# The forget gates' running sums as rows that are split once, and convolution blocks that start two accumulation banks later

## What is computed

```python
qkv = jax.nn.silu(causal_dwconv(jnp.concatenate([gq, gk, gv], axis=-1), gdn_conv[l]))
logf = jax.nn.log_sigmoid((ff + fox_fbias[l]).astype(f32))      # 256 tokens x 4 heads

def fox_attention(q, k, v, logf):
    c = jnp.cumsum(logf, axis=1).transpose(0, 2, 1)
    for i in range(S // Q_BLOCK):                               # two blocks of 128 queries
        s = einsum(q_block, k[:hi]) * scale + (c[:, :, lo:hi, None] - c[:, :, None, :hi])
        p = jax.nn.softmax(jnp.where(mask, s, -jnp.inf), axis=-1)
```

## Time and profile before

| | us |
|---|---|
| executions shown, lowest and highest undisturbed | 1149.84, 1151.31 |
| median shown | 1151.31 |
| the profiled execution, its own time | 1150.2 |
| its span, first to last instruction | 1148.5 |

### The profile page before, as it was taken

One profiled execution on the slowest core, in us unless ns is written; L12 is line 12 of the kernel. 1 busy time (PEld: TensorE's weight loads), 2 busy tenths in 40 slices (PEclk: granted clock), 3 DMA queues, 4 the chain that ended last, 5 costly groups with the idle time before them and its releaser, 6 DMA issues.

```text
span 1148.5 us, 16462 instructions
## 1 busy us (share of the span) xinstructions
PE 1137.1 (99%) x6408; PEld 993.3 (86%) x6408; DVE 741.6 (65%) x931; ACT 589.4 (51%) x788; POOL 105.7 (9%) x162
## 2 busy tenths in 40 slices
PE   9999999999999999999999999999999999999997
PEld 8998888888889999988888898899888888889885
DVE  6866686657777888754664554665866566545465
ACT  5674654446565766543554443564554364444353
POOL 6410211000011000000000000200500010000020
PEclk9999999999999999999999999999999999999999
DMA  9643753455634765564665656465457467555641
GB/s 252 206 156 97 223 185 110 164 201 184 217 132 138 251 207 176 187 215 147 209 214 182 186 174 209 154 213 181 145 187 239 146 229 234 192 168 175 213 137 72
DMA packets 122894, 209.81 MB, mean 183 GB/s; under 512 B 10965, under 2 KB 58186, under 8 KB 122827
## 3 DMA queue, kind: packets, MB, share of 16 engines
q1 hardware_dynamic: 119225, 198.64, 54.2%
q10 hardware_dynamic: 3506, 10.23, 2.4%
q0 software_dynamic: 96, 0.01, 0.1%
HBM read 207.67 MB, written 1.18 MB: 182 GB/s over the span
## 4 chain that ended last, share of the span: by engine, by line
PE 94%; DVE 3%; DMA 1%; ACT 1%; issue 0%; POOL 0%; POOLq 0%; DVEq 0%; SPq 0%; ACTq 0%
PE ACCP L867 28%; PE ACCP L869 28%; PE ACCP L868 28%; PE SMP L1068 3%; DVE CONVF L2301 1%; PE SMP L1061 1%; DVE LO L2176 1%; DMA RAW<-in_w_in_dram 1%; DMA X<-in_x_dram 0%; PE SMP L1221 0%; PE SMP L1237 0%; PE SMP L1021 0%; PE SMP L1016 0%; PE SMP L1015 0%; PE SMP L1406 0%
## 5 line engine op out<-in xcount | busy, mean ns | idle before, releaser
L2176 DVE TENSOR_TENSOR LO<-RAW,HI 128x1024 fp32r<-128x1024 f32 x365 | 438.1, 1237 | 231.3 <-ACT HI L1607 225.0
L1607 ACT ACTIVATE HI<-RAW 128x1024 fp32r<-128x1024 f32 x366 | 370.1, 1054 | 269.6 <-PE ACCP L869 222.6
L867 PE MATMUL ACCP<-HI,XH 128*128 128x512 f32 x704 | 277.4, 394 | 0.0
L869 PE MATMUL ACCP<-HI,XL 128*128 128x512 f32 x704 | 274.4, 390 | 0.0
L868 PE MATMUL ACCP<-LO,XH 128*128 128x512 f32 x704 | 274.0, 389 | 0.0
L867 PE MATMUL ACCP<-XH,HI 128*128 128x256 f32 x640 | 182.0, 284 | 0.7 <-DVE CONVF L2301 0.7
L869 PE MATMUL ACCP<-XH,LO 128*128 128x256 f32 x640 | 181.1, 283 | 0.0
L868 PE MATMUL ACCP<-XL,HI 128*128 128x256 f32 x640 | 181.1, 283 | 0.0
L869 PEld LDWEIGHTS ACCP<-HI,XL 128*128 128x128 f32 x704 | 132.1, 188 | 27.8
L868 PEld LDWEIGHTS ACCP<-LO,XH 128*128 128x128 f32 x704 | 132.3, 188 | 26.2
L867 PEld LDWEIGHTS ACCP<-HI,XH 128*128 128x128 f32 x704 | 132.3, 188 | 26.2
(11 more groups left out here) (416 smaller groups left out, 1144.5 us busy)
## 6 DMA issues: line engine op xcount, KB each, us to landing
RAW<-in_w_in_dram SPq DMA_DIRECT2D x104, 512.0 KB, 4.5
RAW<-in_w_up_dram SPq DMA_DIRECT2D x44, 512.0 KB, 4.4
RAW<-in_ffn_w_gate_dram SPq DMA_DIRECT2D x44, 512.0 KB, 4.6
RAW<-in_ffn_w_up_dram SPq DMA_DIRECT2D x44, 512.0 KB, 4.5
RAW<-in_ffn_w_down_dram SPq DMA_DIRECT2D x44, 512.0 KB, 4.4
RAW<-in_w_down_dram SPq DMA_DIRECT2D x22, 512.0 KB, 4.2
RAW<-in_w_out_dram SPq DMA_DIRECT2D x8, 512.0 KB, 4.4
RAW<-in_w_mkv_dram SPq DMA_DIRECT2D x8, 512.0 KB, 4.3
```

The source lines that it names most:

```text
L867: pe.matmul(dst, lhs[0], rhs[0], start=start, stop=False)
L869: return pe.matmul(dst, lhs[1], rhs[0], start=False, stop=stop)
L1607: act.activation(HI[:, n % RING, half_of(half)], RAW[:, n % RAWS, half, :], ACT.Copy).then_inc(hi_ready, 1)
L2176: dve.tensor_tensor(LO[:, s, c], RAW[:, n % RAWS, half, :], HI[:, s, c].bitcast(f32), ALU.subtract).then_inc(lo_ready[s], 1)
```

## The change

Three things, which don't depend on each other.

**Banks.** gdn block j now uses ACCP bank (j + 2) % 4, so that sbqk blocks 0 to 3 follow gdn blocks 2 to 5. The two products that spread the gain of the first norm go to banks 0 and 1 instead of 2 and 3, the idle spins to bank 2.

**Order on ACT and DVE.** ACT copies block j ahead of the silu of block j-1. DVE adds the taps of block 5 ahead of the LO of block 8; the LO of blocks 8 and 9 follow it.

**Running sums.** DVE builds, early, two small tiles: CUM_IN, log f twice (columns 0 to 3 and 32 to 35), and CUM_SEL, which for each head h has ones in rows h and 32+h. PE forms all running sums once, `fcum`, with two fp32 products behind the join that reads `Z16`. ACT rounds the 36 rows to f32r (CUM), and DVE overwrites rows 32 to 35 with the remainder. In the score stage each head's running sum is then one single-pass product of CUM_SEL (36 rows) with CUM. PE does all single-pass products of the three banks first, then the eight fp32 products of queries and keys. `fcum` is a new name in SMALL, so each name behind it moves one bank on; fS0, fS1a and fS1b now wait for Z16_1, fcum and Tt32_0 instead of Z16_0, Z16_1 and Tt32_0.

```diff
@@ _accumulations @@
-                acc(phase, j, j, (j + (phase == "up") * 2) % 4)
+                acc(phase, j, j, (j + (phase in ("gdn", "up")) * 2) % 4)
@@ SMALL @@
-SMALL += ["Z16_0", "Z16_1", "Tt32_0", "Tt32_1", "fS0", ...
+SMALL += ["Z16_0", "Z16_1", "fcum", "Tt32_0", "Tt32_1", "fS0", ...
@@ tiles @@
+        CUM, CUM_IN = at("CUM", 58, [P, SEQ], f32r), at("CUM_IN", 59, [P, NT, 36])
+        CUM_SEL = at("CUM_SEL", 80, [P, HEADS, P], f32r)
@@ PE @@
             t_half("gate_c", 2, XH, XL)
             join(16, 0)
+            pe.wait_ge(cum_in, 1)
+            small_bank_free(pe, "fcum")
+            pe.matmul(small("fcum")[0:36, 0:SEQ], CUM_IN[:, 0, :], flat(UPTO[:, :, :]), start=True, stop=False)
+            finish(pe.matmul(small("fcum")[0:36, P:SEQ], CUM_IN[:, 1, :], TRI, start=False, stop=True))
             t_half("gate_c", 3, XH, XL)
...
-            def fox_scores(name, t, heads):
+            def fox_bias(name, t, heads):
                 small_bank_free(pe, name)
                 n = (t + 1) * P
                 pe.matmul(by_head(small(name), n), IDENT_R[:, :], every(NEG_AFTER_R[:, SEQ - n:SEQ], len(heads)), start=True, stop=False)
                 for i, h in enumerate(heads):
-                    dst = small(name)[:, i * n:(i + 1) * n]
-                    pe.matmul(dst, FQK[:, h, tok(t)], FQK[:, 4 + h, 0:n], start=False, stop=False)
-                    last = pe.matmul(dst, TS[:, 0, h:h + 1].broadcast_to([P, P]), flat(UPTO[:, 0:t + 1, :]), start=False,
-                                     stop=t == 0 and h == heads[-1])
-                    if t == 1:
-                        last = pe.matmul(dst[:, P:SEQ], TS[:, 1, h:h + 1].broadcast_to([P, P]), TRI, start=False, stop=h == heads[-1])
+                    pe.matmul(small(name)[:, i * n:(i + 1) * n], CUM_SEL[0:36, h, :], CUM[0:36, 0:n], start=False, stop=False)
+
+            def fox_products(name, t, heads):
+                n = (t + 1) * P
+                for i, h in enumerate(heads):
+                    last = pe.matmul(small(name)[:, i * n:(i + 1) * n], FQK[:, h, tok(t)], FQK[:, 4 + h, 0:n], start=False,
+                                     stop=h == heads[-1])
                 finish(last)
+            small_is_taken(pe, "fcum")
+            for scores in SCORES:
+                fox_bias(*scores)
+            for scores in SCORES:
+                fox_products(*scores)
@@ ACT, gdn blocks @@
-                if j:
-                    conv_silu(j - 1)
                 acc_is_done(act, "gdn", Turn(j))
                 (two copies of block j)
+                if j:
+                    conv_silu(j - 1)
                 split_ahead("gdn", Turn(j))
@@ ACT, gate_c @@
             take_small("Z16_0", MB[0:112, 0, :, 0:64], by_head(small("Z16_0")[0:112, 0:256], 64))
+            small_is_done(act, "fcum")
+            copy(CUM[0:36, :], small("fcum")[0:36, 0:SEQ], cum_hi)
@@ DVE, gdn blocks @@
-                split_ahead("gdn", Turn(j))
+                if j < 4:
+                    split_ahead("gdn", Turn(j))
+            split_ahead("gdn", Turn(4))
+            split_ahead("gdn", Turn(5))
@@ DVE, behind the LO of block 19 @@
             split_ahead("foxqk", Turn(3))
+            link(dve.memset(CUM_IN[:, :, :], 0.0))
+            dve.tensor_copy(CUM_IN[:, :, 0:4], TS[:, :, 0:4])
+            dve.tensor_copy(CUM_IN[:, :, 32:36], TS[:, :, 0:4])
+            dve.tensor_tensor(CUM_SEL[0:36, :, :], IDENT[0:36, 0:4]..., IDENT[0:36, 32:36]..., ALU.add).then_inc(cum_in, 1)
             heads_norm(1, XS, 2 * HW)
@@ DVE, gate_c @@
             take_small("Z16_1", MB[0:112, 1, :, 0:64], by_head(small("Z16_1")[0:112, 0:256], 64))
+            dve.wait_ge(cum_hi, 1)
+            dve.tensor_tensor(CUM[32:36, :], small("fcum")[32:36, 0:SEQ], CUM[32:36, :].bitcast(f32), ALU.subtract).then_inc(bank_of("fcum"), 1)
             bias("c", 1)
```

More of the change, by code:

```diff
@@ L148 @@
 SMALL += ["kk0", "kk1", "kq0", "kq1", "z0", "z1", "z2", "z3", "rc0", "rc1", "rc2", "rc3", "so0", "so1", "T16_0", "T16_1", "fTq0", "fTq1", "fTk0", "fTk1"]
-SMALL += ["Z16_0", "Z16_1", "Tt32_0", "Tt32_1", "fS0", "fS1a", "fS1b", "Z32_0", "Z32_1", "T32_0", "T32_1"]
+SMALL += ["Z16_0", "Z16_1", "fcum", "Tt32_0", "Tt32_1", "fS0", "fS1a", "fS1b", "Z32_0", "Z32_1", "T32_0", "T32_1"]
 SMALL += ["Tt64_0", "Tt64_1", "fP0", "fP1a", "fP1b", "fo0", "fo1", "Z64_0", "Z64_1", "T64_0", "T64_1"]
@@ L398, in build @@
         row_max, probs_ready = sems("row_max probs_ready")
+        cum_in, cum_hi = sems("cum_in cum_hi")
         y_hi = sem("y_hi")
@@ L916, in spin @@
                 for _ in range(times):
-                    pe.matmul(ACCP[:, 0, 0:P], ONE_ROW[:, :], ONE_ROW[:, :], start=True, stop=True)
+                    pe.matmul(ACCP[:, 2, 0:P], ONE_ROW[:, :], ONE_ROW[:, :], start=True, stop=True)
             def f_gemm(phase, t, xh, xl, ready=None):
@@ L1098, in _ @@
             for b in range(2):
-                pe.matmul(ACCP[:, 2 + b, :], ONE_ROW[0:97, :], GAIN_ROW[0:97, b * 512:(b + 1) * 512], start=True, stop=True).then_inc(gain_spread, 1)
+                pe.matmul(ACCP[:, b, :], ONE_ROW[0:97, :], GAIN_ROW[0:97, b * 512:(b + 1) * 512], start=True, stop=True).then_inc(gain_spread, 1)
             spin(SPIN_SPREAD)
@@ L1256, in _ @@
                     small_is_taken(pe, f"fT{part}{t}")
-            def fox_scores(name, t, heads):
+            SCORES = (("fS0", 0, range(4)), ("fS1a", 1, (0, 1)), ("fS1b", 1, (2, 3)))
+            def fox_bias(name, t, heads):
                 small_bank_free(pe, name)
@@ L1262, in fox_scores @@
                 for i, h in enumerate(heads):
-                    dst = small(name)[:, i * n:(i + 1) * n]
-                    pe.matmul(dst, FQK[:, h, tok(t)], FQK[:, 4 + h, 0:n], start=False, stop=False)
-                    last = pe.matmul(dst, TS[:, 0, h:h + 1].broadcast_to([P, P]), flat(UPTO[:, 0:t + 1, :]), start=False,
-                                     stop=t == 0 and h == heads[-1])
-                    if t == 1:
-                        last = pe.matmul(dst[:, P:SEQ], TS[:, 1, h:h + 1].broadcast_to([P, P]), TRI, start=False, stop=h == heads[-1])
-                finish(last)
-            fox_scores("fS0", 0, range(4))
-            fox_scores("fS1a", 1, (0, 1))
-            fox_scores("fS1b", 1, (2, 3))
+                    pe.matmul(small(name)[:, i * n:(i + 1) * n], CUM_SEL[0:36, h, :], CUM[0:36, 0:n], start=False, stop=False)
[4 more added lines that the diff above has]
+                                     stop=h == heads[-1])
+                finish(last)
+            small_is_taken(pe, "fcum")
[3 more added lines that the diff above has]
+                fox_products(*scores)
             o_gemm("out_c", 1, y_is_ready())
@@ L2253, in mix_scale @@
                 dve.wait_ge(gain_spread, b + 1)
-                dve.scalar_tensor_tensor(out=XS[:, t, part], in0=X[:, t, part], scalar=root, in1=ACCP[:, 2 + b, :],
+                dve.scalar_tensor_tensor(out=XS[:, t, part], in0=X[:, t, part], scalar=root, in1=ACCP[:, b, :],
                                          op0=ALU.mult, op1=ALU.mult).then_inc(scaled, 1)
@@ L2397, in _ @@
             split_ahead("foxqk", Turn(3))
+            link(dve.memset(CUM_IN[:, :, :], 0.0))
+            dve.tensor_copy(CUM_IN[:, :, 0:4], TS[:, :, 0:4])
+            dve.tensor_copy(CUM_IN[:, :, 32:36], TS[:, :, 0:4])
+            dve.tensor_tensor(CUM_SEL[0:36, :, :], IDENT[0:36, 0:4].unsqueeze(2).broadcast_to([36, HEADS, P]), IDENT[0:36, 32:36].unsqueeze(2).broadcast_to([36, HEADS, P]), ALU.add).then_inc(cum_in, 1)
             heads_norm(1, XS, 2 * HW)
```

## The result

The changed kernel takes 1153.68 us (median of 12 runs, 1151.75 to 1154.4); the kernel before 1150.31. The ratio is 1.0028, 95% interval 1.002 to 1.0036: 3.4 us slower, where 1.0 less was forecast. The profiled execution took 1153.6 us with a span of 1151.9 (before 1148.5).

A forecast was written before the change was run, and what follows sets the result against it. PE, busy in 99% of the span, was taken to bound the kernel. Score stage with `fcum` -1.94, gTk1 -0.16 and gTv0 +1.15 sum to -0.95 from the profiled 1150.2: forecast 1149.3 us, range 1147.6 to 1151.4.

The forecast's parts named there:

- The score stage, "1.94 us saved": Forget-gate part on PE: 3.52 us removed, less 0.92 for single passes and 0.66 for `fcum`; between 1.3 and 2.3 saved.
- The 0.92 for the eight single-pass products: Score stage: four of 128 columns at 0.11 and four of 256 at 0.12, 0.92 us (0.72 to 1.36).
- `fcum` 0.66: Ahead of gate_c block 3: two fp32 products, 0.44 + 0.22 us; 0.5 to 0.85.
- gTk1, 0.16 saved: Convolution part: the second `tiny` read comes at 56.1, so PE starts gTk1 at 56.35 instead of 56.51.
- gTv0, "1.15 us lost": Convolution part: late block 10 loads delay ACT's copy of gTq0, PE waits until 63.75; between 0.25 and 1.55 lost.
- The bound of 4.9 us for a landing: Block 10 loads: land 4.5 us after issue, 3.6 to 4.9; at 4.9 the loss ahead of gTv0 is 1.55 us.
- Rival 3, the clock: PE's clock falls to 1.2 GHz behind the gaps at gTk1 and gTv0, sbqk block 2 doubles: +5.8, 1155.1 us; chance 0.03.
- The first: The block 10 load chain doesn't bite, only the gains stand: 1148.1 us, or 1147.2 without gTk1's wait; chance 0.2.
- The second: Single passes of 128 columns cost 0.22, `fcum` 0.85, waits as forecast or 4.9 long: 1150.1 us, no change; chance 0.15.
- The fourth: A later wait takes back the score stage's saving, as everything behind comes 1.9 us sooner: 1151.2 us; chance 0.05.

The follow-up runs named there:

- experiment 6: The kernel before with the running sums alone, split rows padded with zeros from 36 to 128 rows: 1148.4 us, 0.9985; to 64 rows: 1149.7 us, 0.9998.
- experiment 3: The changed kernel with SP waiting for the second load of block 10 to land before issuing the loads of block 11: 1151.05 us, 1.0007.
- best: The changed kernel with block 8's LO back between taps, `tiny` reads ahead of block 9's LO, and split rows padded to 128: 1146.65 us, 0.9968.

## Why the prediction was wrong

The forecast was a change of -0.95 us, and the trace's account comes to +3.28. Three misses of one size lie between them: the running sums saved 1.39 less, the wait ahead of gTv0 was 1.43 longer, and the fall of the clock, which the sum had at nothing, cost 1.45.

- **The score stage, "1.94 us saved": mis-sized, 0.55.** The 0.92 for the eight single-pass products was 1.45, and the masks between them cost 1.18 instead of 0.69. The step that failed is the reading that their cost goes by columns alone. The row it rested on, joins of 112 and 96 columns, has weights of 128 rows there; I carried it to weights of 36 rows. With 128 rows the net of the whole part came out to the hundredth (experiment 6), where small misses cancel: the eight products cost 0.87 and the masks 0.73. The Trainium skill ("TensorE: Matmul & The Clock Gate", section "LDWEIGHTS (loading the stationary operand)") states that the rows of the weights don't matter to the time of a load. For a load by itself the trace agrees: those of CUM_SEL last 0.186 us with 36 rows and 0.188 with 128. But the pitch of the products depends on them, 0.215 us with 36 or 64 rows and 0.12 with 128, because the low loads start only with their own product. From the time of a load it doesn't follow that the load is hidden, and there I went wrong.
- **`fcum` 0.66: it was 0.91**, beyond the upper bound of 0.85. With 128 weight columns it is 0.65, so fewer columns made it dearer, not cheaper. With 64 it is 0.94 (154.06 to 162.06, less 7.06). The surcharge sits at both turns: from the start of the join to `fcum` it is 1.62 us with 36 columns and 1.53 with 128, from its second product to the next single pass 0.32 and 0.14.
- **gTk1, 0.16 saved: measured 0.20.** The number was right. What it was set against was not: I took the banks to be what let PE go on sooner, and they do nothing; ACT's order moves taps 4 and 5 forward by 1.8 us, which alone gives gTk1 and gTv0 1.8 us. The moved splits then use this up. I costed the edits as one bundle and so never saw that one half of it was worth -1.8 and the other +4.7 to +5.5.
- **gTv0, "1.15 us lost": mechanism right, size off, 2.58.** The wait came where it was forecast, through the chain that was forecast. The bound of 4.9 us for a landing was the step that failed. Once blocks 8 and 9 are freed in one row, four halves are in flight; the second half of block 10 landed about 5.8 us after its issue, near 53.7. With block 11 held back the forecast's 63.75 was measured as 63.67 (experiment 3).
- **Rival 3, the clock, chance 0.03: it happened**, with a price of 1.45 us, not 5.8, since the clock came back after 3.4 us. I excluded it by a window with an idle time of 0.3 us, which says nothing on one of 2.4. It hung on the mis-sized wait: behind 0.98 us the clock didn't fall. The Trainium skill ("TensorE: Matmul & The Clock Gate", section "What's actually happening") has the clock fall with idleness, and here the trace agrees: 0.50 behind a gap of 2.43 us.
- **Rivals 1, 2 and 4.** The first is excluded by ACT's waits of 2.17 and 2.08. The second had the dearer single passes and a dearer `fcum` right, as a surcharge on narrow products and on a change between single pass and fp32; it is one on low or narrow weights. The fourth didn't occur: what is saved or lost up to 183.81 (3.28) is in the span (3.4), and best keeps its gain.

The range was too narrow since all its ends came from rows of an undisturbed kernel: no bound took in that the change brings loads together that had been apart.

What stays open: why PE doesn't start a load of 36 or 64 rows ahead, while those of 112 rows in the join at 165.92 start ahead (165.70) like full ones. The products with low weights also read only 36 or 64 rows of CUM, so no run separates the two operands. It is open too why the clock fell at 64.8 us in one kernel and at 66.2 and 67.9 in two others whose gaps were alike, and whether it would have fallen without the first of the two gaps: no run has the second alone.

## What to carry to other kernels

Cost a reordering edit by edit, also against each other: here one move on ACT was worth 1.8 us, and the two splits moved on DVE beside it threw that away and 2.9 more. When a reordering frees several buffers behind one another, take the landing time of the loads that they release from a stretch where as many are in flight, not from the median. Give the weights of short single-pass products between others full height, padding with zeros where need be, and check in the rows of the weight loads that each starts ahead of its product.

## What the hardware showed that was not expected

- Weights of 36 or 64 rows: single-pass products of 256 columns 0.215 us apart, of 128 columns 0.15; with 128 rows 0.12 and 0.10. A product of 512 columns with full-height weights beside one with low weights moves the next start by 0.32 to 0.43 us instead of 0.23. Their weight loads start together with their own product (173.29), those with 128 rows 0.22 us ahead (168.36 for 168.58). In the forget-gate part this made 1.3 us by the medians (1149.7 with 64 rows, 1148.4 with 128) and 1.39 by the traces. `fcum`, whose weights are 36 or 64 columns wide, shows it too: the load of the first single pass behind it starts at 160.34 for a product at 160.35.
- In idle times of 2.43, 2.28 and 2.15 us or up to 1.4 us behind them, each some 6 us behind the end of another one of 1.39 to 1.95 us, the granted clock went to 1.2 GHz for 3.4 us; it cost 1.45 to 1.55 us in each of the three profiled executions. With 0.98 us in that place it stayed at 2.4 GHz, and with eight spins in the gap as well.
- When two halves of 512 KB are joined by the next block's two, the second of them lands 1.5 us later: 59.56 against 58.08 for the ACT instruction that waits for it. The first is not touched (56.42 against 56.46).
